# Memory's keys and values, computed at the head of the kernel and carried through DRAM to the two cross attentions

## The chip, the cores and the metric

One core of a Trainium2 chip runs the whole program. The metric is the device time of one execution in microseconds (us); the median of three executions is compared. Each execution also has a span, from its first to its last instruction.

## The reference, cut to what matters

Two blocks of two layers each transform 256 tokens of width 1024. The first block also carries 256 context tokens. Each layer of the second block has a cross attention to a fixed memory of 256 rows. Only the lines that the change bears on are shown.

```python
def memory_cross_attention(h, mem_n, w_q, w_kv, w_o):
    q = jnp.einsum("bsd,de->bse", h, w_q).reshape(B, S, 4, 128)
    kv = jnp.einsum("bmd,de->bme", mem_n, w_kv)
    k, v = jnp.split(kv, 2, axis=-1)
    ...
    p = jax.nn.softmax(logits * (XATTN_HEAD_DIM ** -0.5), axis=-1)
    ...

# first block, each layer: mod = silu(c) @ w_mod + b_mod   (shifts, scales and gates of the layer)
# second block, each layer: mem_n = rmsnorm(mem, norm_mem_w[l]), which needs nothing of the layers before
```

So memory's normalised rows, its keys and its values depend on inputs alone. The reference applies the norm's weight per layer; the mean square is the same for both layers.

## The kernel before, in words

**Weights.** All weights pass through one stream of pieces of 1 MB (128 x 2048 numbers), loaded in program order by the queue of SyncE (SP) into a ring of six slots (`load`). Piece n may be loaded once TensorE has counted n-5 pieces as used; a piece counts as used when the first matmul after its last one is issued.

**Split products.** A matrix product in float32 is made of three products in a faster type. ScalarE (ACT) rounds each weight piece to `ring_hi` (L220), VectorE (DVE) writes the rest to `ring_lo` (L223), and TensorE (PE) multiplies high by high, high by low and low by high. `ring_hi` has three slots. `split_ahead` keeps both engines up to two pieces ahead of the product that they take out of PSUM. It stands in `take_products` *ahead of* the copy of the group of outputs with which a new piece begins. An engine works strictly in the order of its instructions, so while it waits for a piece it copies nothing out. A piece holds 256 weight columns: two groups of outputs, each 24 matmuls with 256 columns of tokens. ACT takes the even groups, DVE the odd ones. `pe_products` runs the first four groups (two pieces) side by side, tile by tile of the input.

**Modulation pieces** are used as they are, in float32, eight matmuls each, which the trace shows as sixteen (`pe_mod_piece`), and ACT copies each result row set out (`act_mod_rows`); from the third on, TensorE waits until the piece two before it is copied.

**The head** (`pe_first`, `act_first`, `dve_first`): eight modulation pieces and the mean square of the 512 rows of x and context; then the modulation columns, the norm, and the first big product (`b1_groups`).

**The cross attention of a layer** (`x_groups`, then `x_pairs`): queries are groups 0 to 3 (two pieces), memory's keys groups 4 to 7, its values groups 8 to 11 (four pieces together). Then `phase_end` lets every engine wait for the two others, and `pe_attention` runs four heads in float32. Memory lies in the second half of `xT`; its norm is computed in layer 1's feed-forward of the first block (`pe_mem_mean`, `act_mem_root`, `dve_mem_norm`) and its two parts are split ahead of each mixer's output product (`act_split_mem`, `dve_split_mem`).

Of the kernel before, what the change touches and what calls it, by code (L numbers as in the profile page):

```python
# [22 lines left out]
F32 = mybir.dt.float32  # L23
# [6 lines left out]
P = 128  # L30
# [56 lines left out]
FIRST_SPLITS = (IN_SPLITS, 2 * IN_SPLITS + 4 + 2 * FFN_PIECES)  # L87
# [15 lines left out]
def build(nc, A, y_out):  # L103
    with ExitStack() as ctx:
# [222 lines left out]
        def feature_major(outs, a, b, scale=1.0, rows_=P):  # L327

            res = []
            for c, out in enumerate(outs):  # L330
                terms = [((lambda w, _, k=k, c=c: w[:, k * 256 + c * P:k * 256 + (c + 1) * P]),
                          (lambda _, p, k=k: h(p, k, a, b))) for k in range(KT)]
# [3 lines left out]
        def token_major(outs, first=0, lo=0, n=256, held="new"):  # L336

            res = []
            for i, out in enumerate(outs):
                t0 = (first + i) * P  # L340

                wide = 256 if lo == 0 else n
                terms = [((lambda _, p, k=k, t0=t0: h(p, k, t0, t0 + P)),
                          (lambda w, _, k=k: w[:, k * 256 + lo:k * 256 + lo + wide])) for k in range(KT)]
                res.append((terms, P, wide, copy(out, n), held if i == 0 else "same"))
            return res
# [505 lines left out]

        def pe_first(pe):
            pe.wait_ge(sem("c_cleared"), 1)
            await_next(pe, "c_ready")
            pe.wait_ge(sem("consts_in"), 16)
# [5 lines left out]
            pe_mod_columns(pe, range(EARLY))  # L862

        def act_first(act):
# [4 lines left out]
            act_mod_rows(act, 0)  # L869
            act_mod_rows(act, 1)  # L870
# [489 lines left out]
        def z2(i):  # L1360
            return Zt[:, i, 0:T]
# [537 lines left out]
        rs_mem = c_mat[:, :, :].rearrange("p k s -> p (k s)")  # L1899
# [28 lines left out]
        MEM_SQUARES, MEM_ROOT, MEM_NORMED = 3, 13, 15  # L1928

        def pe_mem_mean(pe, f):  # L1930
            if f == MEM_ROOT - 1:
                pe.wait_ge(sem("mem_summed"), 1)
                mm(pe, bank[4][:, 0:T], const("mean"), hT[:, KT - 1, T:2 * T], start=True, stop=True, last_of="mem_mean")

        def act_mem_root(act, f):
            if f == MEM_SQUARES:
                act.wait_ge(sem("mem_in"), 16)
            if MEM_SQUARES <= f < MEM_SQUARES + KT:
                k = f - MEM_SQUARES
                act.activation(hT[:, k, T:2 * T], xT[:, k, T:2 * T], ACT.Square).then_inc(sem("mem_squared"), 1)  # L1940
            if f == MEM_ROOT:
                act.wait_ge(sem("mem_mean"), 1)
                link(act, act.activation(rs_mem, bank[4][:, 0:T], ACT.Ln, bias=EPS))
                act.activation(rs_mem, rs_mem, ACT.Exp, scale=-0.5).then_inc(sem("mem_root"), 1)
                act.preload_act_table_set("silu_and_others")

        def dve_mem_norm(dve, f):
            k = f - MEM_SQUARES
            if 0 <= k < KT:
                await_next(dve, "mem_squared")  # L1950
            if 0 < k < KT:
                ins = dve.tensor_tensor(hT[:, k, T:2 * T], hT[:, k - 1, T:2 * T], hT[:, k, T:2 * T], ALU.add)
                if k == KT - 1:
                    ins.then_inc(sem("mem_summed"), 1)
                else:
                    link(dve, ins)
            k = f - MEM_NORMED
            if k == 0:
                dve.wait_ge(sem("mem_root"), 1)
            for k in (2 * k, 2 * k + 1) if 0 <= k < KT // 2 else ():  # L1960
                dve.tensor_tensor(xT[:, k, T:2 * T], xT[:, k, T:2 * T], rs_mem, ALU.mult).then_inc(sem("mem_normed"), 1)

        def act_split_mem(act, layer):
            for k in range(KT):
                act.wait_ge(sem("mem_normed"), k + 1)
                act.activation(a_hi[:, k, T:2 * T], xT[:, k, T:2 * T], ACT.Copy, scale=v("norm_mem", layer, k, k + 1))\
                   .then_inc(sem("mem_rounded"), 1)

        def dve_split_mem(dve, layer):
            for k in range(KT):  # L1970
                await_next(dve, "mem_rounded")
                dve.scalar_tensor_tensor(h_lo[:, k, T:2 * T], xT[:, k, T:2 * T], v("norm_mem", layer, k, k + 1),
                                         a_hi[:, k, T:2 * T].bitcast(F32), ALU.mult, ALU.subtract)\
                   .then_inc(sem("late_split"), 1)

# [8 lines left out]
        def _(sp):  # L1984
# [6 lines left out]

            for n in range(2 * SLOTS):
                if n == 2:
                    sp.dma_start(xT[:, :, 0:T], A["xT"]).then_inc(sem("x_in"), 16)
                    sp.dma_start(xT[:, :, T:2 * T], A["ctxT"]).then_inc(sem("x_in"), 16)
                if n == 4:
                    sp.dma_start(vec[:, :], A["vectors"]).then_inc(sem("vectors_in"), 16)
# [3 lines left out]
                if n == EARLY:  # L2001
                    sp.dma_start(cst[:, N_FIRST:N_CONST], A["constants"][:, N_FIRST:N_CONST]).then_inc(sem("rest_in"), 16)
                    sp.dma_start(Z[:, 0:LEVELS * P], A["level_masks"]).then_inc(sem("rest_in"), 16)
# [23 lines left out]
        def _(pe):  # L2027
            for layer in range(DEPTH):
# [14 lines left out]
                pe_ffn(pe, 2 * layer, between=(lambda f: pe_mem_mean(pe, f)) if layer else lambda f: None)  # L2043
# [6 lines left out]
            for layer in range(DEPTH):  # L2050
# [32 lines left out]
        def _(act):  # L2083
            for layer in range(DEPTH):
# [3 lines left out]
                act_rms(act, 0, 0, 2 * T)  # L2088
                if layer == 0:
                    act_apply(act, [b1_segment(0, 0, 0), b1_segment(0, 0, 1)])  # L2090
                else:
                    act_apply(act, [b1_segment(1, 0, 0)])
# [18 lines left out]
                else:  # L2111
                    act_ffn(act, 2, 0, lambda k: v("final1", 0, k, k + 1), lambda f: act_mem_root(act, f))
            for layer in range(DEPTH):
# [16 lines left out]
                act_split_mem(act, layer)  # L2130
# [28 lines left out]
        def _(dve):  # L2159
            for layer in range(DEPTH):  # L2160
# [8 lines left out]
                if layer == 0:  # L2169
                    dve.wait_ge(sem("rest_in"), 48)  # L2170
                    link(dve, dve.tensor_copy(lvl_mask[:, :, :].rearrange("p l n -> p (l n)"), Z[:, 0:LEVELS * P]))
# [20 lines left out]
                else:  # L2192
                    dve_ffn(dve, 2, 0, lambda q: gate_gain(1, 1)(q, 0), n1=2 * T, between=lambda f: dve_mem_norm(dve, f))

            for layer in range(DEPTH):
# [17 lines left out]
                dve_split_mem(dve, layer)  # L2213
# [32 lines left out]
        @block.gpsimd  # L2246
        def _(pool):
            for layer in range(DEPTH):
                pool_sinks(pool, b1_pairs(layer), layer * B1_PHASES // DEPTH + 2)
            pool.dma_start(xT[:, :, T:2 * T], A["memT"]).then_inc(sem("mem_in"), 16)  # L2250
# [3 lines left out]
B1_PHASES = 8  # L2254

# [160 lines left out]
```

## Time and profile before

| | us |
|---|---|
| median of 3 runs | 2810.03 |
| lowest, highest | 2808.38, 2817.32 |
| the profiled execution | 2812.88 |
| its span | 2810.6 |

The profiled execution is 2.3 us longer than its span and 2.85 us above the median. TensorE is busy for 91% of the span, at a mean granted clock of 0.946 of full speed. The chain of work that ended last runs over TensorE for 79% of the span.

### The profile page before, as it was taken

The page shows a single profiled execution, that of the slowest core. Times are in us where ns is not written, and L with a number is a line of the kernel's source. Part 1 is how long each engine was busy: PE and PEld are TensorE (multiplying, and loading weights), DVE is VectorE, ACT ScalarE, POOL GpSimd, SP SyncE. Part 2 cuts the span into 40 slices and gives each one's busy share as a digit, 9 for nine tenths or more (in the row PEclk, how much of TensorE's full clock was granted, in tenths as well). Part 3 has the DMA queues.
Part 4 walks back from the last instruction along what each step waited for, and adds up shares of the span by engine and source line. Part 5 has one row for each costly group of instructions (what it writes and reads, how often), then busy time and mean ns, then how long its engine had stood idle before and what let it go on. Part 6 is the DMA issues. An engine that isn't in the chain of part 4 may idle for free.

```text
span 2810.6 us, 42790 instructions
## 1 busy us (share of the span) xinstructions
PE 2556.6 (91%) x17170; PEld 2262.9 (81%) x17170; DVE 1813.2 (65%) x2484; ACT 1484.5 (53%) x1902; POOL 10.7 (0%) x53
## 2 busy tenths in 40 slices
PE   4988799999999789989698999778899999999997
PEld 3865579999998479989488999668788888888886
DVE  3235956545453575558565546755789888988886
ACT  3226545444341565544555434455577777777775
POOL 0000000000000000000000000000000000000000
PEclk7998899999999799999799999789999999999998
DMA  6242415545443164534033544213599899999994
GB/s 269 90 165 91 180 61 187 187 170 187 170 163 115 54 240 170 186 140 180 16 135 120 183 178 165 90 61 120 198 375 352 333 357 350 353 358 352 353 355 182
DMA packets 80205, 561.56 MB, mean 200 GB/s; under 512 B 8706, under 2 KB 12034, under 8 KB 12435
## 3 DMA queue, kind: packets, MB, share of 16 engines
q1 hardware_dynamic: 79746, 557.86, 52.9%
q8 instruction: 138, 2.26, 0.3%
q0 software_dynamic: 272, 1.05, 0.1%
q14 instruction: 49, 0.39, 0.1%
HBM read 557.82 MB, written 1.05 MB: 199 GB/s over the span
## 4 chain that ended last, share of the span: by engine, by line
PE 79%; DVE 11%; ACT 5%; issue 2%; DMA 1%; SPq 0%; ACTq 0%; PEldq 0%; DVEq 0%; POOL 0%
PE psum L229 78%; DVE ring_lo L223 3%; ACT ring_hi L220 1%; PE psum L634 1%; DVE Z L1411 1%; DVE hT L711 1%; DMA ring<-in_stream 1%; PE psum L1751 1%; ACT hT L675 1%; DVE hT L422 1%; DVE Z L1171 1%; ACT L408 0%; DVE Z L1145 0%; DVE hT L381 0%; DVE Z L1144 0%
## 5 line engine op out<-in xcount | busy, mean ns | idle before, releaser
L223 DVE TENSOR_TENSOR ring_lo<-ring,ring_hi 128x2048 fp32r<-128x2048 f32 x479 | 1097.0, 2291 | 457.0 <-ACT ring_hi L220 453.7
L220 ACT ACTIVATE ring_hi<-ring 128x2048 fp32r<-128x2048 f32 x479 | 916.2, 1914 | 365.6 <-PE psum L229 363.1
L229 PE MATMUL psum<-a_hi,ring_hi 128*128 128x256 f32 (+1 forms) x2448 | 732.1, 299 | 62.0 <-DVE ring_lo L223 20.1
L229 PE MATMUL psum<-a_hi,ring_lo 128*128 128x256 f32 (+1 forms) x2448 | 727.8, 297 | 0.0
L229 PE MATMUL psum<-h_lo,ring_hi 128*128 128x256 f32 (+1 forms) x2128 | 630.2, 296 | 0.0
L229 PE MATMUL psum<-ring_hi,a_hi 128*128 128x512 f32 (+2 forms) x1744 | 538.3, 374 | 5.9 <-DVE h_lo L430 3.7
L229 PEld LDWEIGHTS psum<-a_hi,ring_hi 128*128 128x128 f32 x2448 | 477.4, 195 | 78.8 <-issue 46.7
L229 PEld LDWEIGHTS psum<-a_hi,ring_lo 128*128 128x128 f32 x2448 | 476.8, 195 | 10.3
L229 PEld LDWEIGHTS psum<-h_lo,ring_hi 128*128 128x128 f32 x2128 | 415.9, 195 | 7.4
L229 PEld LDWEIGHTS psum<-ring_hi,a_hi 128*128 128x128 f32 x1744 | 325.8, 189 | 58.3 <-issue 4.1
L229 PE MATMUL psum<-ring_lo,a_hi 128*128 128x512 f32 (+2 forms) x1040 | 370.8, 357 | 0.0
L229 PE MATMUL psum<-Zr,ring_hi 128*128 128x256 f32 x1408 | 255.9, 284 | 8.1 <-DVE xT L579 8.1
L229 PEld LDWEIGHTS psum<-Zr,ring_hi 128*128 128x128 f32 x1408 | 220.7, 193 | 8.9 <-DVE xT L579 8.9
L229 PEld LDWEIGHTS psum<-ring_lo,a_hi 128*128 128x128 f32 x1040 | 197.7, 190 | 28.3
L229 PE MATMUL psum<-ring_hi,Zr 128*128 128x512 f32 x704 | 219.7, 393 | 0.2
L229 PE MATMUL psum<-Zr,ring_lo 128*128 128x256 f32 x704 | 199.8, 284 | 0.0
L229 PE MATMUL psum<-Z 64*128 64x128 f32 (+3 forms) x752 | 124.7, 404 | 66.3 <-DVEq L183 28.2
L540 ACT ACTIVATE mixT<-psum 128x256 f32<-128x256 f32 x88 | 33.7, 383 | 262.9 <-PE psum L229 262.9
L229 PEld LDWEIGHTS psum<-Z 64*128 64x128 f32 (+1 forms) x752 | 77.7, 216 | 96.9 <-issue 35.9
L229 PEld LDWEIGHTS psum<-ring_hi,Zr 128*128 128x128 f32 x704 | 130.0, 188 | 27.7 <-DVE ring_lo L223 1.9
L229 PE MATMUL psum<-ring_lo,Zr 128*128 128x512 f32 x352 | 137.3, 390 | 0.0
L229 PEld LDWEIGHTS psum<-Zr,ring_lo 128*128 128x128 f32 x704 | 135.8, 193 | 0.0
(252 smaller groups left out, 2464.7 us busy)
## 6 DMA issues: line engine op xcount, KB each, us to landing
ring<-in_stream SPq DMA_DIRECT2D x527, 1024.0 KB, 4.9
cst<-in_constants SPq DMA_DIRECT2D x1, 1216.0 KB
xT<-in_xT SPq DMA_DIRECT2D x1, 1024.0 KB, 9.9
xT<-in_ctxT SPq DMA_DIRECT2D x1, 1024.0 KB, 12.1
xT<-in_memT POOLq DMA_DIRECT2D x1, 1024.0 KB, 6.0
out_y<-hT SPq DMA_DIRECT2D x1, 1024.0 KB, 4.8
Z<-in_level_masks SPq DMA_DIRECT2D x1, 448.0 KB
vec<-in_vectors SPq DMA_DIRECT2D x1, 225.0 KB, 11.0
```

Source lines behind the costliest of these rows:

```text
L220: e.activation(hi, raw, ACT.Copy).then_inc(sem("piece_rounded"), 1)
L223: e.tensor_tensor(lo, raw, hi.bitcast(F32), ALU.subtract).then_inc(sem("piece_split"), 1)
L229: ins = pe.matmul(*args, **kw)
L422: ins = dve.scalar_tensor_tensor(hT[:, k, a:b], xT[:, k, a:b], gain(k), rs, ALU.mult, ALU.mult)
L540: act.activation(mixT[:, f % 2, 0:T], bank[2 * (f % 2)][:, 0:T], ACT.Silu)\
L634: ins = pe.transpose(bank[2 + e][:, b * P:(b + 1) * P], s_buf(p, j, e)[:, b * P:(b + 1) * P], const("ident"))
L675: act.activation(s, s, ACT.Exp, bias=neg, accum_out=cols(i, DEN)[:, e:e + 1])\
L711: ins = dve.tensor_tensor_reduce(s_buf(p, i, e)[:, 0:p["nk"]], src, p["mask"], 1.0, p["init"][e], ALU.add, ALU.max, cols(i, MAX)[:, e:e + 1])
L1171: dve.copy_predicated(by_bank(t), mask, grams(t))\
L1411: ins = dve.scalar_tensor_tensor(z2(6 + c), CP[:, c, j:j + T], w, z2(6 + c), ALU.mult, ALU.add)
L1751: ins = pe.transpose(bank[2 + j % 2][:, c * P:(c + 1) * P], hid_tok[j % 2][:, c * P:(c + 1) * P], const("ident"))
```

## The change

Four things are done.

1. The four key and value pieces of each layer move in the stream to the very front, interleaved with the first eight modulation pieces: four pieces for layer 0, four modulation pieces, four pieces for layer 1, four modulation pieces.
2. Memory is loaded first (by SP, not POOL), and its norm, its split for both layers and both products are computed in the head. x and the context are loaded after the fourth piece.
3. POOL stores the results (1 MB for a layer) to a scratch in DRAM, and loads each layer's part back once the phase before the mixer's output product has ended. ACT and DVE wait for both stores before they take the first big product's outputs, and TensorE waits for the load before the cross attention.
4. The cross attention's products are the four query groups alone, and the work on memory in the feed-forward and ahead of the output products is gone.

```diff
 def stream_kinds():
-    return (["mod"] * EARLY + ["split"] * FIRST_SPLITS[0] + ["mod"] * WINDOWS[0]
+    return ((["split"] * KV_SPLITS + ["mod"] * (EARLY // DEPTH)) * DEPTH + ["split"] * IN_SPLITS + ["mod"] * WINDOWS[0]
...
         def pe_first(pe):
+            pe.wait_ge(sem("consts_in"), 16)
+            for k in range(KT):
+                await_next(pe, "mem_squared")
+                mm(pe, bank[4][:, 0:T], const("mean"), mem_squares[:, k, :], start=k == 0, stop=k == KT - 1,
+                   last_of="mem_mean" if k == KT - 1 else None)
+            pe_products(pe, kv_groups(0), "mem_split")
...
-            for m in range(4):
+            for m in range(EARLY // 2):
                 pe_mod_piece(pe, m)
-            pe_norm(pe, 0, 2 * T)
-            for m in range(4, EARLY):
+            for k in range(KT):
+                await_next(pe, "squared")
+                mm(pe, bank[5], const("mean"), hT[:, k, :], start=k == 0, stop=k == KT - 1,
+                   last_of="mean_square" if k == KT - 1 else None)
+            for who in ("act", "dve"):
+                pe.wait_ge(sem(f"product_out_{who}"), KV_SPLITS)
+            pe_products(pe, kv_groups(1), "mem_split")
+            for m in range(EARLY // 2, EARLY):
                 pe_mod_piece(pe, m)
             pe_mod_columns(pe, range(EARLY))
...
+            for k in range(KT):
+                act.activation(mem_squares[:, k, :], memT[:, k, :], ACT.Square).then_inc(sem("mem_squared"), 1)
+            split_ahead(act, "act", 0)
+            await_next(act, "mem_mean")
+            link(act, act.activation(rs_mem, bank[4][:, 0:T], ACT.Ln, bias=EPS))
+            act.activation(rs_mem, rs_mem, ACT.Exp, scale=-0.5).then_inc(sem("mem_root"), 1)
+            act.wait_ge(sem("vectors_in"), 16)
+            act_split_mem(act, 0)
+            act_split_mem(act, 1)
+            take_products(act, "act", kv_groups(0))
             act.wait_ge(sem("x_in"), 32)
             act_squares(act, 0, 2 * T)
-            for m in range(2, EARLY):
+            for m in range(EARLY // 2):
+                act_mod_rows(act, m)
+            take_products(act, "act", kv_groups(1))
+            for m in range(EARLY // 2, EARLY):
                 act_mod_rows(act, m)
...
-            for j in range(2):
-                g += feature_major([z2(4 + 2 * j), z2(5 + 2 * j)], T, 2 * T)
-            for j in range(2):
-                g += token_major([tok[:, t * 768 + 256 * j:t * 768 + 256 * (j + 1)] for t in range(2)], 2)
             return g
...
-                pe_products(pe, x_groups(layer), "h_split", late=4)
+                pe_products(pe, x_groups(layer), "h_split")
                 phase_end(pe)
+                pe.wait_ge(sem("kv_in"), 32 * (layer + 1))
                 pe_attention(pe, x_pairs())
...
+                for who in ("act", "dve"):
+                    pool.wait_ge(sem(f"product_out_{who}"), KV_SPLITS * (layer + 1))
+                pool.dma_start(A["kv"][layer], kv_out[layer]).then_inc(sem("kv_stored"), 16)
...
+            for layer in range(DEPTH):
+                for other in ("pe", "act", "dve"):
+                    pool.wait_ge(sem(f"phase_{other}"), FOX_PHASES[layer])
+                pool.dma_start(Zt[:, 4:8, 0:T], A["kv"][layer][:, 0:1024].rearrange("p (h n) -> p h n", h=4))\
+                    .then_inc(sem("kv_in"), 16)
```

ScalarE's order in the head. `c_mat` is the modulation's input, `rows_a` the copied rows of a modulation piece, `hT<-xT` a square of x, `ring_hi` a rounded weight piece, `Z<-psum` a group of outputs copied out, `a_hi` the norm's high part. Before:

```order
L867 ACTIVATE c_mat<-c_in 128x8x2
L823 ACTIVATE rows_a<-psum 128x256 x2
L369 ACTIVATE hT<-xT 128x512 x8
L823 ACTIVATE rows_a<-psum 128x256 x6
L407 ACT_TABLE_LOAD
L407 ACTIVATE mixT<-psum 128x512
```

And now, from the third new piece of layer 0's product (`kv_groups(0)`) to the norm of x:

```order
L221 ACTIVATE ring_hi<-ring 128x2048
L302 ACTIVATE Z<-psum 128x256
L221 ACTIVATE ring_hi<-ring 128x2048
L302 ACTIVATE Z<-psum 128x256
L370 ACTIVATE hT<-xT 128x512 x8
L824 ACTIVATE rows_a<-psum 128x256 x4
...
L302 ACTIVATE Z<-psum 128x256
L824 ACTIVATE rows_a<-psum 128x256 x4
L408 ACT_TABLE_LOAD
L408 ACTIVATE mixT<-psum 128x512
```

The squares of x and each four modulation rows now stand behind a product's last roundings and copies; in the part left out are layer 1's four roundings and the copies between them.

VectorE's order from the queries' groups (`TENSOR_SCALAR`) of a cross attention to its first read of scores (`ISA`). Before:

```order
L305 TENSOR_SCALAR Z<-psum 128x256
L223 TENSOR_TENSOR ring_lo<-ring,ring_hi 128x2048
L305 TENSOR_SCALAR Z<-psum 128x256
L223 TENSOR_TENSOR ring_lo<-ring,ring_hi 128x2048
L303 COPY Z<-psum 128x256
...
L223 TENSOR_TENSOR ring_lo<-ring,ring_hi 128x2048
L303 COPY tok<-psum 128x256
L711 ISA hT,sc<-psum,cst 128x256
```

And now:

```order
L224 TENSOR_TENSOR ring_lo<-ring,ring_hi 128x2048
L306 TENSOR_SCALAR Z<-psum 128x256
L224 TENSOR_TENSOR ring_lo<-ring,ring_hi 128x2048
L306 TENSOR_SCALAR Z<-psum 128x256
L712 ISA hT,sc<-psum,cst 128x256
```

The four pairs of a rest of a weight piece and a copy of keys or values are gone, and the last rest now stands directly ahead of the last copy before the phase ends.

## Rows read from the trace of the kernel before

**Rows 1.** The page, part 1: TensorE's busy time, share of the span, instructions.
```profile
PE 2556.6 (91%) x17170; PEld 2262.9 (81%) x17170; DVE 1813.2 (65%) x2484; ACT 1484.5 (53%) x1902; POOL 10.7 (0%) x53
```

**Rows 2.** Timeline of the head, all engines: start, us, engine, instruction, count [idle before].
```profile
7.10 1.94 PE L229 MATMUL psum<-ring,c_mat 128*32 128x256 f32 x16 [7.10 <-DMA ring<-in_stream]
...
15.50 4.26 ACT L369 ACTIVATE hT<-xT 128x512 f32<-128x512 f32 x8 [4.01 <-DMA xT<-in_ctxT]
...
18.01 1.94 PE L229 MATMUL psum<-ring,c_mat 128*32 128x256 f32 x16 [6.99 <-DMA ring<-in_stream]
...
22.39 7.96 PE L229 MATMUL psum<-hT,cst 128*128 128x512 f32 x16
...
30.27 3.66 PE L229 MATMUL psum<-ring,c_mat 128*32 128x256 f32 x64
...
34.40 1.28 ACT L407 ACT_TABLE_LOAD   x1
...
34.44 4.02 PE L229 MATMUL psum<-cst,rows_a 128*128 128x2 f32 x32 [0.50 <-ACT rows_a L823]
...
40.98 0.88 DVE L432 SCALAR_TENSOR_TENSOR h_lo<-hT,modT,a_hi 128x256 fp32r<-128x256 f32 x2 [0.18 <-ACT a_hi L417]
...
58.58 0.77 PE L229 MATMUL psum<-a_hi,ring_hi 128*128 128x512 f32 x1 [20.13 <-DVE ring_lo L223]
```

**Rows 3.** The page, part 6: DMA issues, last number is us to landing.
```profile
ring<-in_stream SPq DMA_DIRECT2D x527, 1024.0 KB, 4.9
...
xT<-in_memT POOLq DMA_DIRECT2D x1, 1024.0 KB, 6.0
```

**Rows 4.** Window in the head; the last three are PEclk, DMA share, GB/s.
```profile
20.00:25.00 5.00, 4.48 (x20) 1.81 (x21) 0.00 (x0) 0.77 (x2) 0.00 (x0) 0.59 1.03 428
```

**Rows 5.** Timeline of ScalarE before and in the first cross attention's products.
```profile
1409.91 3.29 ACT L1966 ACTIVATE a_hi<-xT,vec 128x256 fp32r<-128x256 f32 x8
...
1450.19 1.92 ACT L220 ACTIVATE ring_hi<-ring 128x2048 fp32r<-128x2048 f32 x1 [0.16 <-PE psum L229]
```

**Rows 6.** Timeline of VectorE at the same place, to the first score read.
```profile
1452.14 2.29 DVE L223 TENSOR_TENSOR ring_lo<-ring,ring_hi 128x2048 fp32r<-128x2048 f32 x1 [1.70 <-ACT ring_hi L220]
1454.35 0.42 DVE L305 TENSOR_SCALAR Z<-psum 128x256 f32<-128x256 f32 x1
...
1473.77 0.42 DVE L303 COPY tok<-psum 128x256 f32<-128x256 f32 x1 [1.34 <-PE psum L229]
1475.23 0.42 DVE L711 CUSTOM_DVE_ANT_0 hT<-psum,cst 128x256 f32<-128x256 f32 x1 [1.04 <-PE psum L229]
```

**Rows 7.** The chain that ended last, same place: start, us, what.
```profile
1437.62 36.12 PE psum L229 x288
...
1486.71 0.38 ACT mixT L688
```

**Rows 8.** Timeline of TensorE at the end of the values and the start of the attention.
```profile
1473.33 0.28 PE L229 MATMUL psum<-ring_hi,h_lo 128*128 128x256 f32 x1
1473.45 0.28 PE L229 MATMUL psum<-ring_lo,a_hi 128*128 128x256 f32 x1
1474.38 1.10 PE L229 MATMUL psum<-Z 128*128 128x256 f32 x4 [0.66 <-DVEq L183]
```

**Rows 9.** Short windows around idle stretches of TensorE; columns as in rows 4.
```profile
1437.00:1437.50 0.50, 0.00 (x0) 0.00 (x0) 0.45 (x2) 0.41 (x2) 0.00 (x0) 0.70 0.63 262
...
1388.00:1389.00 1.00, 1.00 (x4) 0.82 (x4) 0.00 (x0) 0.16 (x2) 0.00 (x0) 0.50 0.00 0
...
1894.50:1895.00 0.50, 0.00 (x0) 0.01 (x1) 0.50 (x2) 0.32 (x1) 0.00 (x0) 0.58 0.32 131
```

**Rows 10.** Timeline of TensorE at the end of two idle stretches.
```profile
1377.49 0.80 PE L229 MATMUL psum<-Z 64*128 64x128 f32 x4 [7.10 <-DVEq L183]
...
1437.62 0.55 PE L229 MATMUL psum<-a_hi,ring_hi 128*128 128x256 f32 x1 [3.72 <-DVE h_lo L430]
```

**Rows 11.** Timeline of TensorE in layer 1's first feed-forward: memory's mean.
```profile
1127.11 0.60 PE L229 MATMUL psum<-hT,cst 128*128 128x256 f32 x2
```

More of the change, by code:

```diff
@@ L331, in feature_major, with token_major @@
                 terms = [((lambda w, _, k=k, c=c: w[:, k * 256 + c * P:k * 256 + (c + 1) * P]),
-                          (lambda _, p, k=k: h(p, k, a, b))) for k in range(KT)]
+                          (lambda _, p, k=k: of(p, k, a, b))) for k in range(KT)]
                 res.append((terms, rows_, b - a, copy(out, b - a, scale), "new" if c == 0 else "same"))
             return res
-        def token_major(outs, first=0, lo=0, n=256, held="new"):
+        def token_major(outs, first=0, lo=0, n=256, held="new", of=h):
             res = []
@@ new lines, in build, with kv_groups @@
+        rs_mem = mixT[:, 1, 0:T]
+        masks_in = Z[:, 10240:10240 + LEVELS * P]
+        kv_out = [Z[:, 6144 + 2048 * l:8192 + 2048 * l] for l in range(DEPTH)]
+        def kv_groups(layer):
+            of = lambda part, k, a, b: mem_parts[layer][part][:, k, a:b]
+            keys = kv_out[layer][:, 0:1024].rearrange("p (h n) -> p h n", h=4)
+            values = kv_out[layer][:, 1024:2048].rearrange("p (t n) -> p t n", t=2)
+            g = []
+            for j in range(2):
+                g += feature_major([keys[:, 2 * j, :], keys[:, 2 * j + 1, :]], 0, T, of=of)
+            for j in range(2):
+                g += token_major([values[:, t, 256 * j:256 * (j + 1)] for t in range(2)], of=of)
+            return g
@@ L864, in act_first, with dve_split_mem @@
+        def dve_split_mem(dve, layer):
+            hi, lo = mem_parts[layer]
+            for k in range(KT):
+                await_next(dve, "mem_rounded")
+                dve.scalar_tensor_tensor(lo[:, k, :], memT[:, k, :], v("norm_mem", layer, k, k + 1),
+                                         hi[:, k, :].bitcast(F32), ALU.mult, ALU.subtract).then_inc(sem("mem_split"), 1)
         def act_first(act):
@@ L877, in dve_first @@
             dve.memset(c_mat[:, :, :], 0.0).then_inc(sem("c_cleared"), 1)
-            dve.wait_ge(sem("vectors_in"), 16)
+            split_ahead(dve, "dve", 0)
+            dve.wait_ge(sem("mem_in"), 16)
+            dve.wait_ge(sem("mem_root"), 1)
+            for k in range(KT):
+                dve.tensor_tensor(memT[:, k, :], memT[:, k, :], rs_mem, ALU.mult).then_inc(sem("mem_normed"), 1)
+            dve.wait_ge(sem("vectors_in"), 16)
+            dve.wait_ge(sem("mem_normed"), KT)
+            dve_split_mem(dve, 0)
+            dve_split_mem(dve, 1)
+            take_products(dve, "dve", kv_groups(0))
+            take_products(dve, "dve", kv_groups(1))
             await_next(dve, "mod_columns")
@@ L1947, in dve_mem_norm @@
[L1947 to L1974, printed above, removed]
@@ L2042, in _ @@
                 pe_mean(pe, 5, (5, 6, 7), 0, n)
-                pe_ffn(pe, 2 * layer, between=(lambda f: pe_mem_mean(pe, f)) if layer else lambda f: None)
+                pe_ffn(pe, 2 * layer)
                 if layer == 0:
@@ L2087, in _ @@
                     act_first(act)
-                act_rms(act, 0, 0, 2 * T)
+                act_rms(act, 0 if layer else 5, 0, 2 * T)
                 if layer == 0:
                     act_apply(act, [b1_segment(0, 0, 0), b1_segment(0, 0, 1)])
+                    act.wait_ge(sem("kv_stored"), 32)
                 else:
@@ L2192, in _ @@
                 else:
[L2193 removed]
+                    dve_ffn(dve, 2, 0, lambda q: gate_gain(1, 1)(q, 0), n1=2 * T)
             for layer in range(DEPTH):
@@ L2336 @@
     mods = np.concatenate([by_columns(i["w_mod"][l]) for l in range(DEPTH)], 0)
+    for l in range(DEPTH):
+        pieces += [by_columns(i["xattn_w_kv_2"][l]), mods[l * EARLY // DEPTH:(l + 1) * EARLY // DEPTH]]
     heads = np.array([64 * h + k for t in range(4) for h in (t, t + 4) for k in range(64)])
@@ L2344 @@
         if l == 0:
-            pieces += [mods[0:EARLY], by_columns(w), mods[EARLY:EARLY + MOD_PIECES], by_columns(out)]
+            pieces += [by_columns(w), mods[EARLY:EARLY + MOD_PIECES], by_columns(out)]
         else:
```

67 lines of the change are left out of this document (34 added, 33 removed).

## The prediction

> **What bounds the kernel now.** I read the page first. TensorE is busy for 2556.6 of 2810.6 us [rows 1], so what is left to win lies in the stretches in which it stands still or runs at half its clock; other engines' work matters only where TensorE waits for it.
>
> The head is such a stretch. In the timeline [rows 2] the first big product begins at 58.58 after 20.13 us of idle, and before that TensorE does only eight modulation pieces, a mean and the columns. In the window 20 to 25 the DMA engines are full at 428 GB/s: a piece of 1.05 MB takes 2.5 us [rows 4].
>
> The other place is the cross attention. The chain shows TensorE alone from 1437.62 for 36.12 us, 288 matmuls [rows 7]: 96 for the queries, 192 for keys and values. Two starts stand 0.12 us apart [rows 8], so keys and values take 192 x 0.12 = 23.0 us of path in a layer. The change moves 46 us of work from a place where it is all path to one where TensorE idles. The question is how much of it the head can really hide.
>
> **The saving in a cross attention.** Before, the values end at 1473.75, VectorE copies the last group at 1473.77, and reads the first score at 1475.23 [rows 6]. The queries end 23.0 us earlier, at 1450.7. But the last copies of the queries stand behind a piece to be split: ScalarE rounds one from 1450.19 (1.92 us) [rows 5], VectorE writes its rest from 1452.14 (2.29 us) and only then copies, 1454.35 to 1454.77 [rows 6]. Today this hides behind the keys. Now the phase ends there. From the end of the last copy (1474.19) to the read (1475.23) are 1.04 us, so the read comes at 1455.81, 19.4 us earlier instead of 23.0.
>
> Then the clock. TensorE now idles from 1450.7 to about 1455.0, 4.3 us. Today it idles for 3.72 us ahead of the queries' first matmul at 1437.62 [rows 10], and in the half microsecond from 1437.0 the granted clock is 0.70, on its way from full to half; at the same place of the other layer, from 1894.5, it is 0.58 [rows 9]. So the attention should begin at 1.2 GHz. A dense product gets it back soon: 36.12 us are 1.6 more than 288 x 0.12, which is what some 3 us at half clock cost. The sparse float32 work of another attention began at 1377.49 after 7.10 us of idle [rows 10] and still ran at 0.50 from 1388 to 1389 [rows 9]. The four score steps are 1.10 us each at full clock [rows 8] and stand on the path one after the other, with the transposes behind them. At half clock they cost 4 x 1.1 = 4.4 us more, and the first transposes a few tenths: I take 4.8. The bounds are 0 (the clock stays) and about 10 (half clock through the whole attention, which takes 12.3 us, 1474.38 to 1486.71, some of it not TensorE's). Saving a layer: 19.4 - 4.8 = 14.6, both layers alike: 29.2 us, between 19 and 39.
>
> The rest that goes is hidden today. The splits of memory (3.29 us on ScalarE from 1409.91 [rows 5]) run while TensorE works on the output product. The norm in the feed-forward lies under TensorE too; only its mean, two records in 0.60 us [rows 11], is on the path: 0.4 us. The load from DRAM is hidden: POOL issues it before the output product, over 40 us ahead of its use, and a load on POOL's queue took 6.0 us [rows 3].
>
> **The cost at the head.** I follow the new order with durations of [rows 2, 3, 5], and 0.38 for a copy of 128 x 256 out of PSUM [rows 7].
>
> To the first product: memory takes the place of the first piece and lands at 7.1. Eight squares at about 0.33 bring ScalarE to 9.8; it rounds pieces 0 and 1 (the second lands near 12.0) until 13.9; logarithm, table load and exponential are 0.38 + 1.28 + 0.42: 16.0. VectorE has its two rests at 16.2, normalises eight tiles by 18.9 and gives the first split at 19.4. A split takes 0.41 (3.29 / 8), a TensorE step of twelve matmuls 1.44, so TensorE is not held again. Layer 0's eight groups are 192 x 0.12 = 23.0, and 1.5 more because 2.9 us of them are at half clock: 43.9.
>
> First fetch: at its third piece ScalarE has to split piece 8 of the stream, which lies in the slot of piece 2, and at its fourth piece 9, in the slot of piece 3. Piece 3 is released by the first modulation matmul, at 43.9. Landing takes 4.9 [rows 3], rounding 1.9, the copy that was held 0.4: 51.1. Behind it on ScalarE stand the squares of x (4.26) and the first modulation row (0.38): 55.8. TensorE had done two modulation pieces by 45.7 and waits for that row: 10 us of new idle, so the clock is half again. Two pieces at 1.94: 59.7. The mean of x, 8.0: 67.7. Layer 1's groups, 23.0: 90.7.
>
> Second fetch, the same again for piece 17 in the slot of piece 11: 4.9 + 1.9 + 0.4 + 0.4 = 7.6, 98.3. Two modulation pieces at 1.94, a row 0.4, the columns 4.0: 106.6. From the columns' end (38.46) to the first finished split of x (40.98 + 0.88) are 3.4 us: 110.0. Here something is won, and it is in the figure: today the product waits on for its weights' rests until 58.58, while now two pieces have been split long before. It then goes at the pace of TensorE.
>
> The product starts at 110.0 instead of 58.6: 51.4 us later. Bounds: landing in 4.2 instead of 4.9, modulation pieces at full clock (3.66 / 4 = 0.92 each, [rows 2]) and memory 3 us earlier give 43; landings as slow as POOL's 6.0 each, and columns at half clock, give 58.
>
> The stores don't count. The second begins near 100 and takes about 6.0 us by its nearest row [rows 3]; ScalarE asks for it only after the norm's eight tiles, 9.5 us after the product's start, at 119.5. The constants and masks (1.7 MB, 4 us at 428 GB/s) stand ahead of piece 12 on SP, which TensorE wants at 91. POOL's copies of the sinks stand behind the stores and are wanted only in the attention after the big product.
>
> **The sum.** 51.4 - 29.2 - 0.4 = +21.8 us. Against the profiled execution (span 2810.6, time 2812.9) that is a span of 2832.4 and a time of 2834.7; the median of the runs was 2.85 below the profiled one: 2831.8, so 2832. A measurement of this kernel tells about 0.3% from no change, 8.4 us.
>
> **The rivals.**
>
> The head goes at TensorE's pace. Then neither fetch holds a modulation row: the waits of 10.1 and 6 us go, and the four modulation pieces run at 0.92 instead of 1.94, 4.1 less. The product starts at about 90, 31 us later, and the sum is +1: not slower. It decides if pieces 8, 9, 16 and 17 are in SBUF when ScalarE comes to them. For it speaks that the DMA engines are idle from 28 us on; against it, that the wait is for a slot and not for bandwidth. Chance 0.12; together with a kept clock (-8.3) 0.04.
>
> The clock stays at 2.4 GHz through the new idle stretch. Savings of 19.4 twice: +12.2. For it: 4.3 us is not much more than 3.72. Against it: in both layers the clock fell before that stretch was over [rows 9]. Chance 0.12.
>
> The clock stays at half through the whole attention. Savings of about 9.4 twice: +32.2. For it speaks the other attention [rows 9, 10], which ran at half clock for over 10 us; against it, that its steps had been preceded by a longer idle stretch. The Trainium skill, in TensorE: Matmul & The Clock Gate, Part 4 (transposes), says that transposes don't count as the array's work for the clock in the way that matmuls do. By that rule the attention's sixteen transposes would not help it back to full clock, and this rival's +32 would be the result; whether this attention comes back to full clock before its end no run shows yet. Chance 0.15.
>
> A new wait (`kv_stored`, `kv_in`) shows. It needs a store of over 19 us or a load of over 40; each would add what exceeds that. Chance 0.02. The forecast has 0.55.
>
> **How the numbers follow.** Slower by over 0.3%: forecast, both clock rivals and the wait, less a little for a head and a saving at their good bounds together (43 - 39 = +4): 0.81. Within 0.3%: 0.13. Faster: 0.06. The range leaves the first rival below it and reaches up through the low clock with a slow head (58 - 19 = +39): 2812 to 2849. The forecast's own is 2824 to 2840.
>
> **What would show it.** In the head: TensorE idle for about 10 us after the second modulation piece and 6 us after the sixth, each ended by ScalarE's row, and behind it the landing of a piece; the first matmul with 512 moving columns at 110. In each cross attention: 96 matmuls, then about 4.3 us of idle ended by VectorE's copy, a clock of 0.5 after it, and the attention some 5 us longer than 12.3. Wrong would be: idle stretches missing in the head, or keys and values' 23 us saved in full.

## The result, and the profile after

| | median, us | lowest, highest | ratio to before, 95% interval |
|---|---|---|---|
| before, run beside it | 2819.14 | 2806.65, 2825.81 | |
| changed | 2840.75 | 2827.59, 2849.39 | 1.0084 [1.0064, 1.0105] |

By the ratio the changed kernel is slower by 0.84%, about 24 us; the two medians of the table lie 21.6 us apart. Its profiled execution has a span of 2839.1 us against 2810.6, 28.5 more; TensorE is busy for 2582.0 us instead of 2556.6 [rows 1]. The prediction was 2832 us, +21.8. It was added to 2810.03, the median of the first three runs of the kernel before; over all twelve that median is 2819.14. These 9.1 us of the starting point are why the absolute time came out 8.8 us above 2832 while the difference came out close.

The page after, parts 1 and 6:

```profile
PE 2582.0 (91%) x17184; PEld 2283.1 (80%) x17184; DVE 1811.8 (64%) x2477; ACT 1482.9 (52%) x1901; POOL 14.5 (1%) x58
...
ring<-in_stream SPq DMA_DIRECT2D x527, 1024.0 KB, 4.8
kv_scratch<-Z POOLq DMA_DIRECT2D x2, 1024.0 KB, 6.8
...
Z<-kv_scratch POOLq DMA_DIRECT2D x2, 512.0 KB, 4.5
tok<-kv_scratch POOLq DMA_DIRECT2D x2, 512.0 KB, 5.6
```

**The head after.** First what TensorE waits for there (the list of waits, 0 to 125 us: total, times, longest):

```profile
PE psum L230 <- ACT rows_a L824: 17.0, 3, 10.3
PE psum L230 <- ACT Z L921: 7.3, 1, 7.3
PE psum L230 <- DVE Zr L910: 6.5, 1, 6.5
PE psum L230 <- DVE h_lo L433: 3.5, 1, 3.5
```

Then the chain that ended last in the same stretch (start, us, what):

```profile
19.60 26.29 PE psum L230 x197
...
45.90 4.80 DMA ring<-in_stream
...
50.72 1.91 ACT ring_hi L221
...
52.91 4.15 ACT hT L370 x8
57.06 0.28 ACT rows_a L824
...
57.47 35.13 PE psum L230 x245
...
92.76 4.75 DMA ring<-in_stream
...
97.53 1.91 ACT ring_hi L221
...
99.72 0.28 ACT rows_a L824
```

And TensorE's timeline behind it, at the two rows that answer to the last ones of [rows 2]:

```profile
104.27 4.42 PE L230 MATMUL psum<-cst,rows_a 128*128 128x2 f32 x32 [0.49 <-ACT rows_a L824]
112.17 0.77 PE L230 MATMUL psum<-a_hi,ring_hi 128*128 128x512 f32 x1 [3.47 <-DVE h_lo L433]
```

Read the waits first: the largest, 17.0 us, names ScalarE's copy of a modulation row. The chain says what that means: the copy itself takes 0.28 us, and ahead of it on ScalarE stand the rounding of a stream piece (1.91) and a DMA that began only when layer 0's keys and values were done (45.90). The first big product starts at 112.17 where it started at 58.58: 53.6 us later. The four waits add up to 34.3 us. Before, the same list for 0 to 62 us gives 20.1 us behind VectorE's rest of a piece, 15.2 behind the stream and 0.5 behind a row, 35.8 in all, with the stretches of 20.13, 7.10, 6.99 and 0.50 of [rows 2] in it:

```profile
PE psum L229 <- DMA ring<-in_stream: 15.2, 4, 7.1
```

So TensorE idles nearly as long as before: of the 46 us of products that moved there, next to nothing was hidden. Outside these waits the head holds 77.9 us of TensorE's work where it held 22.8, 55.1 more. The two products are 48.7 of it, since part of the first ran at half clock, and the mean of memory, which stands here now, is 5.8:

```profile
7.27 5.81 PE L230 MATMUL psum<-Z,cst 128*128 128x256 f32 x16 [7.27 <-ACT Z L921]
```

**The first cross attention after.** Timelines of ScalarE, VectorE and TensorE, three fences. A score step is one of the four groups of matmuls in the attention (`psum<-Z`, four records):

```profile
1505.89 1.91 ACT L221 ACTIVATE ring_hi<-ring 128x2048 fp32r<-128x2048 f32 x1 [0.16 <-PE psum L230]
...
1526.62 0.38 ACT L689 ACTIVATE mixT<-psum 128x256 f32<-128x256 f32 x1 [0.51 <-PE psum L230]
```

```profile
1507.83 2.29 DVE L224 TENSOR_TENSOR ring_lo<-ring,ring_hi 128x2048 fp32r<-128x2048 f32 x1 [1.70 <-ACT ring_hi L221]
1510.04 0.41 DVE L306 TENSOR_SCALAR Z<-psum 128x256 f32<-128x256 f32 x1
```

```profile
1510.60 2.05 PE L230 MATMUL psum<-Z 128*128 128x256 f32 x4 [4.22 <-DVEq L184]
1513.17 2.08 PE L230 MATMUL psum<-Z 128*128 128x256 f32 x4 [0.53 <-DVE sc L712]
1515.78 2.08 PE L230 MATMUL psum<-Z 128*128 128x256 f32 x4 [0.53 <-DVE sc L712]
...
1520.24 0.66 PE L635 MATMUL psum<-cst,hT 128*128 128x128 f32 x4
```

The windows over it (the three numbers at the end are PEclk, DMA share, GB/s):

```profile
1508.00:1510.00 2.00, 0.00 (x0) 0.00 (x0) 2.00 (x1) 0.07 (x1) 0.00 (x0) 1.00 0.98 414
1510.00:1512.00 2.00, 1.40 (x3) 1.18 (x4) 0.48 (x3) 0.00 (x0) 0.00 (x0) 0.50 0.04 16
...
1520.00:1522.00 2.00, 1.79 (x14) 1.36 (x12) 1.35 (x8) 1.07 (x4) 0.00 (x0) 0.94 0.00 0
```

VectorE's copy of the last queries' group (1510.04) comes behind the rest of a new piece (2.29 us), as before [rows 6]. TensorE idles for 4.22 us, the granted clock reads 0.50 (1.2 GHz) behind it, and three score steps take 2.05 to 2.08 us instead of 1.10 [rows 8]. At 1520 to 1522 the clock is back. From the first queries' matmul (1493.30, the chain) to the first score step are 17.30 us, before 1437.62 to 1474.38 [rows 8, 10], 36.76: 19.46 won. From that step to the last copy of ScalarE are 16.02 us (1526.62), before 12.33 (1486.71 [rows 7]): 3.69 lost. The second layer repeats it, 4.22 us of idle and 16.05.

**Where the difference stands along the program.** Starts of the same instructions in both traces, after less before. The layers are those of the second block, and the mark of an output product is VectorE's first `mix_lo` for it:

| place | before | after | difference |
|---|---|---|---|
| first big product | 58.58 | 112.17 | +53.6 |
| mixer's output product, layer 0 | 1407.98 | 1463.66 | +55.7 |
| cross attention's output product, layer 0 | 1487.81 | 1528.07 | +40.3 |
| mixer's output product, layer 1 | 1865.40 | 1906.78 | +41.4 |
| cross attention's output product, layer 1 | 1945.19 | 1971.01 | +25.8 |
| span | 2810.6 | 2839.1 | +28.5 |

Head +53.6, cross attentions -15.4 and -15.6 in these marks, and +5.9 in the stretches between, from which the change takes nothing but memory's norm and splits: 2.1, 1.1 and 2.7. The 2.7 lie behind the last cross attention, where the clock differs. TensorE's timeline at the start of the next product, before:

```profile
1994.64 0.73 PE L229 MATMUL psum<-ring_hi,a_hi 128*128 128x512 f32 x2 [2.15 <-DVE a_hi L1740]
```

And after:

```profile
2021.81 1.07 PE L230 MATMUL psum<-ring_hi,a_hi 128*128 128x512 f32 x2 [2.15 <-DVE a_hi L1808]
```

The same two matmuls behind the same wait take 1.07 us instead of 0.73: the granted clock reads 0.50 from 2022 to 2025, and before it reads 1.00 from 1995 to 1999. From the last mark to the end are 865.4 us before and 867.9 to 868.3 in all seven other traces, the changed kernel's and those of the experiments. So these 2.7 us go with the moved or missing keys and values and are no accident of one execution; why the clock differs there stays open. Over all runs the whole difference is about +24, and how the 5.9 us look in them no trace shows.

### The profile page after: what moved, and what is told of

It reads as the page before. It is cut to its first block, busy times and chain, and to the rows that moved or that the text cites. A ratio compares the mean times of both kernels' runs of the same rounds, so it can differ in the third digit from the quotient of the medians.

```text
span 2839.1 us, 42816 instructions
## 1 busy us (share of the span) xinstructions
PE 2582.0 (91%) x17184; PEld 2283.1 (80%) x17184; DVE 1811.8 (64%) x2477; ACT 1482.9 (52%) x1901; POOL 14.5 (1%) x58
## 4 chain that ended last, share of the span: by engine, by line
PE 80%; DVE 10%; ACT 6%; issue 2%; DMA 0%; ACTq 0%; PEldq 0%; DVEq 0%; SPq 0%
PE psum L230 78%; DVE ring_lo L224 3%; ACT ring_hi L221 1%; PE psum L635 1%; DVE Z L1483 1%; DVE hT L712 1%; PE psum L1819 1%; ACT hT L676 1%; DVE Z L1243 0%; ACT L409 0%; DVE hT L423 0%; DMA ring<-in_stream 0%; DVE hT L382 0%; DVE Z L1216 0%; DVE Z L1217 0%
## 5 line engine op out<-in xcount | busy, mean ns | idle before, releaser
L230 PE MATMUL psum<-a_hi,ring_lo 128*128 128x256 f32 (+1 forms) x2384 | 708.8, 297 | 0.0
L230 PE MATMUL psum<-h_lo,ring_hi 128*128 128x256 f32 (+1 forms) x2064 | 611.5, 296 | 0.0
L230 PEld LDWEIGHTS psum<-a_hi,ring_lo 128*128 128x128 f32 x2384 | 463.8, 195 | 10.3
L230 PEld LDWEIGHTS psum<-h_lo,ring_hi 128*128 128x128 f32 x2064 | 402.6, 195 | 7.5
L230 PE MATMUL psum<-ring_lo,a_hi 128*128 128x512 f32 (+2 forms) x976 | 353.0, 362 | 0.0
L230 PE MATMUL psum<-Zr,ring_hi 128*128 128x256 f32 x1472 | 272.7, 288 | 14.6 <-DVE xT L580 8.1
L230 PEld LDWEIGHTS psum<-Zr,ring_hi 128*128 128x128 f32 x1472 | 235.1, 197 | 15.8 <-DVE xT L580 8.9
L230 PE MATMUL psum<-ring_hi,Zr 128*128 128x512 f32 (+1 forms) x768 | 231.3, 384 | 0.1
L230 PEld LDWEIGHTS psum<-ring_lo,a_hi 128*128 128x128 f32 x976 | 185.5, 190 | 28.4
L230 PEld LDWEIGHTS psum<-Z 64*128 64x128 f32 (+1 forms) x752 | 83.5, 229 | 104.3 <-issue 43.9
L230 PE MATMUL psum<-ring_lo,Zr 128*128 128x512 f32 (+1 forms) x384 | 146.4, 381 | 0.0
```

Of the source, the lines that this page charges most:

```text
L230: ins = pe.matmul(*args, **kw)
```

## The experiments

All kernels are variants of the changed one except "no keys and values", which is a variant of the kernel before. The theory: the head pays the moved products in full plus two waits in which ScalarE, bound to its order, stands before a piece whose slot is not yet free; and each cross attention gives back 19.4 us less a clock that fell in the wait for the queries' copy. Rivals: the waits are TensorE's pace or bandwidth in disguise, and the half clock belongs to the attention itself.

| run | median, us | ratio to before, 95% interval | span | first big product |
|---|---|---|---|---|
| changed | 2840.75 | 1.0084 [1.0064, 1.0105] | 2839.1 | 112.17 |
| first fetch off | 2832.69 | 1.0069 [1.0046, 1.0091] | 2830.9 | 101.88 |
| head unblocked | 2822.42 | 1.0017 [1.0001, 1.0034] | 2819.2 | 92.51 |
| copy before split | 2822.82 | 1.0026 [1.0008, 1.0044] | 2827.9 | as changed |
| clock kept | 2831.76 | 1.0040 [1.0017, 1.0063] | 2834.3 | as changed |
| both mended | 2800.49 | 0.9937 [0.9917, 0.9958] | 2797.3 | 93.57 |
| no keys and values | 2783.57 | 0.9889 [0.9861, 0.9917] | 2790.4 | 58.64 |

The kernel before that ran beside them had a median of 2814.05 (first fetch off, head unblocked, copy before split, no keys and values) and of 2821.22 (clock kept, both mended). The spans are of one execution each.

### First fetch off

```diff
             act_split_mem(act, 1)
-            take_products(act, "act", kv_groups(0))
+            take_products(act, "act", kv_groups(0), upto=KV_SPLITS)
...
-            take_products(dve, "dve", kv_groups(0))
+            take_products(dve, "dve", kv_groups(0), upto=KV_SPLITS)
```

While they take layer 0's keys and values, ScalarE and VectorE split no piece beyond those that this product needs.

> The changed kernel, but in layer 0's key and value product at the head the two engines that split weights stop at its own four pieces, so ScalarE no longer waits for pieces 8 and 9 of the stream ahead of the squares of x and the modulation rows. Theory (the waits for a ring slot's next piece, on an engine that works in order, hold TensorE): the idle stretch of 10.3 us after the second modulation piece goes, the four modulation pieces and the mean run closer to full clock, and the first big product starts at 100 instead of 112.2 us; the time falls by about 12 us against the changed kernel (ratio to the kernel before about 1.004). Rival (the head is held by DMA bandwidth or by the splitting work itself): pieces 4 and 5 of the products are then split late, layer 1's product waits for them, and the big product still starts at 110 to 113; the time does not move by more than 2 us.

Measured: the first big product at 101.88, 10.3 us earlier. The ratio fell to 1.0069 [1.0046, 1.0091]; 1.004 was expected, so of the 12 us some 4 show in the runs and 8.2 in the span. 1.9 us of the span's shortfall lie between the first big product and the mixer of layer 0; the rest of the miss is open. TensorE's timeline at the second fetch:

```profile
87.28 3.64 PE L230 MATMUL psum<-ring,c_mat 128*32 128x256 f32 x32 [6.24 <-ACT rows_a L824]
91.42 6.99 PE L230 MATMUL psum<-cst,rows_a 128*128 128x2 f32 x32 [0.49 <-ACT rows_a L824]
101.88 0.77 PE L230 MATMUL psum<-a_hi,ring_hi 128*128 128x512 f32 x1 [3.48 <-DVE h_lo L433]
```

The wait of 10.3 us is gone and the second one, untouched, is 6.24 us as before. So the first was the order on ScalarE. The columns took 6.99 us here, at a granted clock of 0.50 from 91 on, and 4.42 in the changed kernel, where it was 1.00 from 104 to 106. So the clock took back 2.6 us: the gain ahead of the columns was 12.9.

### Head unblocked

```diff
-            take_products(act, "act", kv_groups(0))
+            take_products(act, "act", kv_groups(0), upto=KV_SPLITS)
...
+            split_ahead(act, "act", 0)
+            act_rms(act, 5, 0, 2 * T)
-            take_products(act, "act", kv_groups(1))
+            take_products(act, "act", kv_groups(1), upto=2 * KV_SPLITS)
+            split_ahead(act, "act", 0, upto=2 * KV_SPLITS + 1)
...
+            split_ahead(act, "act", 0)
...
-            take_products(dve, "dve", kv_groups(0))
-            take_products(dve, "dve", kv_groups(1))
+            take_products(dve, "dve", kv_groups(0), upto=KV_SPLITS)
+            split_ahead(dve, "dve", 0)
+            take_products(dve, "dve", kv_groups(1), upto=2 * KV_SPLITS)
+            split_ahead(dve, "dve", 0)
```

The same for both fetches, with x's norm moved ahead of layer 1's copies.

> The same for both products at the head: neither splits beyond its own pieces; the root of x's mean square is taken before layer 1's product; of the first big product's two pieces one is split ahead of the last four modulation rows and one behind them. Theory: both idle stretches (10.3 and 6 us) go, TensorE runs from the first key matmul to the columns nearly without a break, and the big product starts at 93 (91 to 96) instead of 112.2; the time falls by 17 to 20 us against the changed kernel, ratio to the kernel before 1.0015 (0.9995 to 1.003). Rival (bandwidth or splitting work): start at 105 or later, ratio 1.006 or more.

Measured: 92.51, and 2822.42 us. The waits of TensorE, 0 to 125 us:

```profile
PE psum L230 <- ACT Z L921: 7.2, 1, 7.2
PE psum L230 <- DVE h_lo L433: 6.4, 1, 6.4
PE psum L230 <- DVE Zr L910: 6.1, 1, 6.1
PE psum L230 <- ACT rows_a L824: 0.7, 2, 0.5
```

Against the changed kernel's list, the 17.0 us behind ScalarE's rows are 0.7. The new order is worth 19.7 us of the 53.6: the waits are 13.9 us shorter in all, and the other 5.8 us are work of TensorE that goes faster. The head still costs 33.9: of 46 us moved, 12 are hidden. One fetch still stands in the way, and the wait behind `h_lo` is 2.9 us longer by it (6.4 for 3.5); the chain:

```profile
78.88 6.02 DMA ring<-in_stream
...
86.86 2.29 DVE ring_lo L224
```

VectorE writes that piece's rest ahead of the modulation's columns and so holds the norm. So 12 is what this order hides, not the most that could be hidden.

### Copy before split

```diff
-                take_products(act, "act", x_groups(layer))
+                take_products(act, "act", x_groups(layer), upto=wanted["act"] + 1)
...
+                split_ahead(act, "act", 0)
...
-                take_products(dve, "dve", x_groups(layer))
+                take_products(dve, "dve", x_groups(layer), upto=wanted["dve"] + 1)
...
+                split_ahead(dve, "dve", 0)
```

In each cross attention the last queries' groups are copied before the next product's piece is split; ScalarE splits it behind the phase's end, VectorE behind the attention.

> The changed kernel, but in each cross attention the second piece of the output projection is no longer split ahead of the last copies of the queries: ScalarE rounds it after the phase's end, VectorE writes its rest after the attention. Theory (the phase's end waits for 1.9 + 2.3 us of splitting, and the idle of 4.2 us lets the clock fall): TensorE idles for about 1 us, its clock stays at full, the first score is read 1.5 us after the queries' end instead of 5.6, and the attention takes 12.3 us instead of 16; 7.8 us a layer, 15 to 16 us in all, ratio to the kernel before 1.003. Rival 1 (only the wait, the clock falls for another reason): 8 us in all, clock 0.5 at the attention's start, ratio 1.0055. Rival 2 (the split is merely moved and is paid ahead of the output projection): less than 4 us in all, ratio 1.007 or more.

Measured: 2822.82 us, 1.0026 [1.0008, 1.0044], where 1.003 was expected. VectorE's and then TensorE's timeline at the end of the queries, two fences:

```profile
1514.87 0.42 DVE L306 TENSOR_SCALAR Z<-psum 128x256 f32<-128x256 f32 x1 [3.91 <-PE psum L230]
1515.58 0.42 DVE L306 TENSOR_SCALAR Z<-psum 128x256 f32<-128x256 f32 x1 [0.29 <-PE psum L230]
```

```profile
1516.15 1.10 PE L230 MATMUL psum<-Z 128*128 128x256 f32 x4 [0.61 <-DVEq L184]
```

TensorE's idle falls from 4.22 to 0.61 us, and the first score step takes 1.10 us: the granted clock reads 1.00 in every 2 us from 1513 to 1523. From the first queries' matmul (1502.47) to the first score step are 13.68 us, 3.6 less than 17.30; from there to ScalarE's last copy (1528.48) 12.33 instead of 16.02. That is 7.3 us a layer, half of it the wait and half the clock; 7.8 was expected. The run alone can't tell the two halves apart, since it removed both.

### Clock kept

```diff
                 pe_products(pe, x_groups(layer), "h_split")
+                for _ in range(4):
+                    mm(pe, bank[7], const("mean"), cst[:, 0:512], start=True, stop=True)
```

Four products that nobody reads are put between the queries and the wait. The wait for VectorE's copy stays as it is. The kernel computes all that the reference asks for.

> The changed kernel with four float32 products of 512 columns put on TensorE behind the last product of the queries in each layer, ahead of its wait for their copy; their results are used by nothing. The wait itself (4.2 us in the changed kernel, for a queries' copy that stands behind a first matmul's split) stays, since it is not TensorE's. If the 1.20 GHz at the attention's start comes from the empty stretch in front of it, the granted clock reads 1.00 there, the four head products fall from 2.08 us to about 1.05, and each layer is about 4 us shorter: ratio near 1.0055 against the kernel before, the changed one being 1.0084. Rival: the attention's own sparse work keeps the clock down whatever stands in front; then it still reads 0.50 there, nothing is gained, and the ratio stays at 1.008.

Measured: 2831.76 us, 1.0040 [1.0017, 1.0063], below the 1.0055 that was expected but with it in the interval. The clock's two times 3.69 us make 0.26%, so the median gained more than the marks explain. TensorE's timeline:

```profile
1515.14 3.60 PE L230 MATMUL psum<-cst 128*128 128x512 f32 x8
1519.52 1.10 PE L230 MATMUL psum<-Z 128*128 128x256 f32 x4 [0.78 <-DVEq L184]
```

From the first queries' matmul (1502.23) to the first score step are 17.29 us, the changed kernel's 17.30: the wait is untouched. From there to ScalarE's last copy (1531.85) are 12.33 instead of 16.02, in both layers. So 3.69 us a layer are the clock alone. With the stretch ahead filled it stays at 1.00 from 1513 to 1525; so it was the empty stretch that let it fall, and the attention's own sparse work doesn't bring it down. The rival falls.

### No keys and values

```diff
-            for j in range(2):
-                g += feature_major([z2(4 + 2 * j), z2(5 + 2 * j)], T, 2 * T)
-            for j in range(2):
-                g += token_major([tok[:, t * 768 + 256 * j:t * 768 + 256 * (j + 1)] for t in range(2)], 2)
...
-                act_split_mem(act, layer)
...
-                dve_split_mem(dve, layer)
...
-                    [by_columns(i["xattn_w_kv_2"][l]), by_columns(i["xattn_w_o_2"][l], 512)]
+                    [by_columns(i["xattn_w_o_2"][l], 512)]
```

The kernel before, without memory's keys, values, their weights and memory's norm; its cross attentions read what happens to lie in those buffers. It shows the saving without the head.

> The kernel before with the keys, values and norm of memory left out altogether (its eight pieces gone from the stream; the cross attentions read what lies in the tiles), so it is the saving of the change without its price at the head. Theory, by the changed kernel's trace: 15.4 us less in each cross attention and 0.4 for the mean, 31 us in all, ratio 0.989, with 46 us of TensorE's work gone; the clock at the start of each attention is 0.5. Rival (the saving is nearer to the 46 us of work, and later stretches give back what the change cost elsewhere): 40 us or more, ratio 0.986 or less. Rival 2 (the 8 MB less of weights also relieve the DMA queues in the last stretch): more than 40 us with the extra behind 2000 us.

Measured: 2783.57 us, 0.9889 [0.9861, 0.9917], about 31 us less, as expected. The chain in the first cross attention:

```profile
1467.20 1.37 PE psum L229 x4
...
1469.08 2.09 PE psum L229 x4
```

Here too the attention begins behind a wait for the queries' copy (4.26 us), and the clock is at half from its second score step on: from mixer to cross attention 64.3 us (1418.58 to 1482.92), as in the changed kernel (1463.66 to 1528.07, 64.4), against 79.8 before. Removing 46 us of products from the path gives 31, wherever they go. Of the other 15 some 7 are the waits for the queries' copy, which the products had covered, and nearly all the rest is TensorE at half clock around these waits.

### Both mended

> Both mendings in one kernel: the head with the first fetches' splits taken out of the way of the memory's norm, and the queries' copies ahead of the next product's split in both cross attentions. If the two costs are separate they add: 19.7 us less in the head (the first big matmul at about 92.5) and 7.4 us less in each cross attention (about 57 us from the mixer's last split to the cross attention's, against 79.8 before), together 34 us less than the changed kernel and 10 us less than the kernel before: ratio 0.996, between 0.994 and 0.998. Rival: the clock or the weights' stream takes one of them back, and the ratio stays at 1.000 or above.

It has the edits of "head unblocked" and "copy before split" together. Measured: 2800.49 us, 0.9937 [0.9917, 0.9958]: faster than the kernel before by 0.63%, about 18 us. Expected were 0.996 and a range from 0.994: the kernel is a little faster than the two costs explain. The first big product and the chain in the first cross attention, two fences:

```profile
93.57 0.76 PE L230 MATMUL psum<-a_hi,ring_hi 128*128 128x512 f32 x1 [5.20 <-DVE h_lo L433]
```

```profile
1472.10 13.09 PE psum L230 x96
...
1485.78 0.68 PE psum L230 x2
```

Head 18.6 us less than the changed kernel, cross attentions (1442.46 to 1499.57, 57.1, and 56.7) 14.8 less: 33.4, where 34 was expected. The profiled execution is 41.8 shorter; the other 8.4 lie in stretches that neither edit touches. 5.7 of them stand between the cross attention of layer 0 and the mixer's output product of layer 1 (373.0 us against 378.7), among them the mixer's sparse work. Changed kernel, then this one:

```profile
1848.00:1856.00 8.00, 6.36 (x22) 4.52 (x22) 4.65 (x24) 1.82 (x7) 0.00 (x0) 0.50 0.00 0
```

```profile
1820.00:1828.00 8.00, 5.05 (x34) 3.57 (x36) 6.82 (x39) 3.57 (x13) 0.00 (x0) 0.92 0.01 2
```

The same work runs at 0.50 in one and 0.92 in the other. "Copy before split" and "clock kept" have 373.0 and 372.4 us there too, "first fetch off" and "head unblocked" 378.7 and 378.8, the kernel before 377.6 and the one without keys and values 375.0. So the short stretch is seen in the three kernels whose attention was freed of its half clock, but the kernel before had no half clock there either. Why the clock differs 300 us behind the edits wasn't tried; it stays open.

## Why the prediction was right

**The direction and the sum.** +21.8 us predicted, about +24 measured over all runs, +28.5 in the profiled execution. In the profiled execution the terms of the forecast come to 53.6 - 31.0 = 22.6, against 51.4 - 29.2 = 22.2; the head was 2.2 too small and the savings 1.8 too small, and that these two errors nearly cancel is luck. The forecast put everything else at nothing but the 0.4 for memory's mean, which no run separates; there the marks show +5.9, 2.7 of it in all seven traces.

**The head: 51.4 predicted, 53.6 measured.** Each step is in the chain. The first keys start at 19.60 (19.4); the first fetch is a DMA of 4.80 behind the last use of its slot, 1.91 of rounding, and the squares (4.9, 1.9, 4.26); TensorE's new idle stretches are 10.28 and 6.24 us (10 and 6); the second fetch begins at 92.76, lands in 4.75 and lets TensorE go at 100.13 (98.3). The error is in small terms: layer 0's product ended at 45.2 (the modulation piece behind it begins at 45.25 in the timeline) instead of 43.9 (its half-clock part was longer: the matmuls stand closer only from 25.26 on, 5.7 us behind their start, where 2.9 were taken), 0.5 us of releases at the second fetch, and 0.4 in the columns.

**The rival "at TensorE's pace"** was priced at a product start of 90, and "head unblocked" reached 92.51 once the order on ScalarE was changed. It failed on the ground given: the wait is for a slot and an order. In the changed kernel the DMA moves 3 GB/s from 75 to 80 us. What I had named for the rival, DMA engines idle from 28 us on, holds in neither trace: before, they move 415 GB/s from 28 to 31; in the changed kernel they rest from 28 to 34 only and move 303 from 34 to 37.

**The saving: 14.6 a layer predicted, 15.4 and 15.6 measured.** The earlier read, 19.4, measured 19.46. The clock was the term that was off: 4.8 predicted, 3.69 measured by "clock kept". The first three score steps took 0.95 us more each, which puts the start of the fourth 2.9 us later, and only 0.8 came from there on, the fourth step among it: I had put all four on the path. The other 0.35 is a later first split of the output product (1.45 us behind ScalarE's last copy instead of 1.10).

**The clock rivals.** "Stays at 2.4 GHz" needed the clock to survive 4.22 us of idle; it read 1.00 until 1510 and 0.50 from there. "Half through the whole attention" is refuted by the window of 1520 to 1522, 0.94. The Trainium skill's rule in TensorE: Matmul & The Clock Gate, Part 4, that transposes don't count for the clock as matmuls do, stood beside that rival of +32. Here the clock came back 9.7 us into the attention, at the end of the fourth score step, behind the first of four sets of transposes (0.51 from 1520.00 to 1520.25, 1.00 from there to 1520.50). So the rival is refuted and the rule is not: no run separates the transposes from the score matmuls around them.

**No new wait:** the stores landed in 6.8 us and the loads in 4.5 and 5.6 (the page after, part 6), and none ends a wait of TensorE.

## What to carry to other kernels

Before moving work into idle time, ask what that idle time is made of: here 35.8 us of idle were waits in a chain of other engines and transfers, and 46 us of moved products left 34.3. An in-order engine that fetches ahead must not stand before a transfer whose slot the moved work itself still holds; two such stretches cost 16.5 us, and a new order of prefetches, copies and norm gave back 19.7. And where work leaves the path, look at what it covered: a copy behind a split cost 3.6 us of wait a layer and, by the empty stretch that it left, 3.7 us of clock.

## What the runs showed of the hardware that was not expected

**The same dense work ran at either clock, behind the same wait.** In the profiled execution of "clock kept" TensorE waits for 1.53 us, to 899.64, and then:

```profile
905.00:910.00 5.00, 5.00 (x25) 5.00 (x25) 0.29 (x1) 0.00 (x0) 0.00 (x0) 0.50 0.00 0
...
920.00:925.00 5.00, 5.00 (x25) 5.00 (x25) 2.19 (x1) 2.19 (x2) 0.00 (x0) 0.50 0.48 195
```

The changed kernel at the same work, behind a wait as long (1.52 us, to 901.05):

```profile
905.00:910.00 5.00, 5.00 (x47) 5.00 (x46) 0.00 (x0) 0.28 (x1) 0.00 (x0) 1.00 0.00 0
```

For over 20 us TensorE is busy without a gap and does 25 matmuls in 5 us instead of 47. From the first big product to the mixer of layer 0 the trace with it has 1361.3 us and the changed kernel's 1351.5, so it costs some 10 us. "Copy before split" and "no keys and values" had it in their profiled executions too, the other five did not. Each kernel has one trace, so no pair of traces shows both clocks in one kernel. That it changes from execution to execution is an inference: the runs of "clock kept" go from 2821.41 us at a mean granted clock of 0.952 to 2841.37 at 0.942, and its profiled one took 2836.05 at 0.947. The stretch is over 0.3% of the kernel, so a single span can't be read as the effect of an edit; the marks along the program can, in the stretches that they bound.
